# The pitch and the place of the split weight tiles in a two-layer decoder step

## What is computed

```python
def _layer(x, ...):
    x = _layernorm(DN_ALPHA * x + 0.5 * _swiglu(x, ffn1_wg, ffn1_wu, ffn1_wd), ln1_g, ln1_b)
    m, ... = _mixer(x, ...)
    x = _layernorm(DN_ALPHA * x + m, ln2_g, ln2_b)
    x = _layernorm(DN_ALPHA * x + 0.5 * _swiglu(x, ffn2_wg, ffn2_wu, ffn2_wd), ln3_g, ln3_b)

def _swiglu(x, wg, wu, wd):
    return (jax.nn.silu(x @ wg) * (x @ wu)) @ wd

def _mixer(x, ...):
    z = x @ w_in
    cv, cb, cc, lx, lg, q, gl = jnp.split(z, IN_OFFSETS, axis=-1)
    y_conv = (cb * conv3(cc * cv)) @ conv_out
    y_lru = (rg_lru(conv4(lx)) * jax.nn.gelu(lg)) @ lru_out
    y_att = attention(q, k_mem, v_mem) @ att_out
    merged = g[:, :, 0] * y_conv + g[:, :, 1] * y_lru + g[:, :, 2] * y_att
    return merged @ w_o, ...
```

## Time and profile before

| | us |
|---|---|
| median of 3 runs | 1476.64 |
| lowest and highest of them | 1473.49, 1476.66 |
| the profiled execution | 1473.8 |
| its span | 1472.0 |
| PE busy | 1435.8 |
| DVE busy | 880.0 |
| ACT busy | 640.3 |

### The profile page before, as it was taken

One profiled execution on the slowest core, in us unless ns is written; L12 is line 12 of the kernel. 1 busy time (PEld: TensorE's weight loads), 2 busy tenths in 40 slices (PEclk: granted clock), 3 DMA queues, 4 the chain that ended last, 5 costly groups with the idle time before them and its releaser, 6 DMA issues.

```text
span 1472.0 us, 25592 instructions
## 1 busy us (share of the span) xinstructions
PE 1435.8 (98%) x10700; PEld 1420.6 (97%) x10700; DVE 880.0 (60%) x1128; ACT 640.3 (43%) x825; POOL 29.2 (2%) x62
## 2 busy tenths in 40 slices
PE   7999999999999999999999999999999999999996
PEld 7999998999999989999989999999999999999996
DVE  4555557586655775554575555576775557655544
ACT  4444445344334564443464444453623345534433
POOL 1000000000000000000000000000000000000000
PEclk9999999999999999999999999999999999999998
DMA  6444445544535544444444444444454544444451
GB/s 249 169 171 171 158 158 168 193 170 161 211 144 170 196 146 160 156 169 160 171 155 161 169 171 158 158 158 172 147 211 145 188 143 144 172 166 154 168 176 54
DMA packets 39565, 243.60 MB, mean 165 GB/s; under 512 B 4529, under 2 KB 4545, under 8 KB 15809
## 3 DMA queue, kind: packets, MB, share of 16 engines
q1 hardware_dynamic: 32976, 219.30, 42.6%
q0 software_dynamic: 5936, 22.01, 4.2%
q10 hardware_dynamic: 576, 1.18, 0.2%
HBM read 238.97 MB, written 3.50 MB: 165 GB/s over the span
## 4 chain that ended last, share of the span: by engine, by line
PE 91%; DVE 5%; issue 1%; ACT 1%; DMA 1%; DVEq 0%; SPq 0%; ACTq 0%; POOLq 0%
PE ps L370 27%; PE ps L372 27%; PE ps L371 27%; PE ps L542 2%; PE ps L551 2%; PE ps L409 1%; PE ps L414 1%; PE ps L410 1%; DVE wlo L877 1%; DVE y L1026 1%; DVE y L1034 1%; ACT whi L650 1%; DMA raw<-in_ffn_wu 1%; DVE xl L1042 1%; PE ps L557 1%
## 5 line engine op out<-in xcount | busy, mean ns | idle before, releaser
L877 DVE TENSOR_TENSOR wlo<-raw,whi 128x1024 fp32r<-128x1024 f32 x448 | 510.8, 1146 | 372.0 <-ACT whi L650 371.9
L650 ACT CAST whi<-raw 128x1024 fp32r<-128x1024 f32 x448 | 440.1, 985 | 575.6 <-PE ps L372 494.2
L370 PE MATMUL ps<-xh,whi 128*128 128x288 f32 x1984 | 591.3, 298 | 0.2 <-DVE pool L935 0.2
L372 PE MATMUL ps<-xh,wlo 128*128 128x288 f32 x1984 | 586.5, 296 | 0.0
L371 PE MATMUL ps<-xl,whi 128*128 128x288 f32 x1984 | 586.1, 295 | 0.0
L370 PEld LDWEIGHTS ps<-xh,whi 128*128 128x128 f32 x1984 | 373.9, 188 | 1.0 <-issue 0.4
L371 PEld LDWEIGHTS ps<-xl,whi 128*128 128x128 f32 x1984 | 373.9, 188 | 0.6
L372 PEld LDWEIGHTS ps<-xh,wlo 128*128 128x128 f32 x1984 | 373.9, 188 | 0.0
L370 PE MATMUL ps<-hh,whi 128*128 128x288 f32 (+1 forms) x1088 | 323.9, 298 | 0.0
L372 PE MATMUL ps<-hh,wlo 128*128 128x288 f32 (+1 forms) x1088 | 320.0, 294 | 0.0
L371 PE MATMUL ps<-hl,whi 128*128 128x288 f32 (+1 forms) x1088 | 319.8, 294 | 0.0
(11 more groups left out here) (169 smaller groups left out, 881.8 us busy)
## 6 DMA issues: line engine op xcount, KB each, us to landing
raw<-in_w_in SPq DMA_DIRECT2D x48, 1024.0 KB, 4.9
raw<-in_ffn_wu SPq DMA_DIRECT2D x44, 1024.0 KB, 4.8
raw<-in_ffn_wg SPq DMA_DIRECT2D x43, 1024.0 KB, 4.8
raw<-in_ffn_wd SPq DMA_DIRECT2D x32, 1024.0 KB, 4.9
raw<-in_ffn_wd SPq DMA_DIRECT2D x16, 768.0 KB, 4.2
pool<-in_cache_k POOLq DMA_DIRECT2D x16, 512.0 KB, 4.5
pool<-in_cache_v POOLq DMA_DIRECT2D x16, 512.0 KB, 4.8
raw<-in_w_o SPq DMA_DIRECT2D x8, 1024.0 KB, 5.1
```

The costliest lines, as they stand in the source:

```text
L370: mm(out, wh, mh, start=start, stop=False)
L372: return mm(out, wl, mh, start=False, stop=stop)
L650: s_.copy(whi[:, s, k0:k1, :], raw[:, s, k0:k1, :]).then_inc(hi_ready, 1)
L877: return v.tensor_tensor(out, full, high.bitcast(F32), sub)
```

## The change

```diff
@@ -17,6 +17,7 @@
 ATANH_TERMS = 9
 WARM = 20
+SHIFT = 24
@@ -126,8 +127,10 @@
         raw = sb("raw", [P, 2, 8, BC])
-        whi = sb("whi", [P, 2, 8, BC], F32R)
-        wlo = sb("wlo", [P, 2, 8, BC], F32R)
+
+        whi = sb("whi", [P, 2, 8, T], F32R)[:, :, :, 0:BC]
+        wlo = sb("wlo", [P, 2, 8, T], F32R)[:, :, :, 0:BC]
+        sb("shift", [P, SHIFT])
         x = sb("x", [P, KD, T])
```

## The result

| | before | changed |
|---|---|---|
| median, us | 1476.5 (4 runs) | **1463.6** (4 runs, 1461.9 to 1468.2) |
| ratio to before | | **0.9917**, 95% interval 0.9902 to 0.9932 |
| profiled execution, us | 1473.8 | 1468.2 |
| its span, us | 1472.0 | 1466.4 |
| granted clock, share of 2.4 GHz | 0.992 | 0.990 |

The change makes the kernel 0.8% faster, 13 us. My likeliest case, no change at 1476 us, did not come; the time lies in the stated range, and within 1.5 us of what I had given to the rival "the distance counts, and 96 is good".

What follows compares the result with a forecast made beforehand. The matrix engine was taken as the bound, busy 1435.8 of 1472.0 us, so time is matmul count times pace. Splits, loads, pitch and the 96 bytes each counted 0, giving 1476 us, likeliest range 1472 to 1480, overall 1453 to 1489.

Steps and rivals of the forecast that it cites:

- no change at 1476 us: Whole kernel: the layout changes but the matmul pace does not; 1476 us, chance 0.42.
- the distance counts, and 96 is good: 288-column matmuls: all reach the better of two paces, 131.7 ns, giving 1465 us or less; chance 0.36 for better distance.
- 0 for the splits: Weight casts on ScalarE and subtractions on VectorE: unchanged within 2 ns at 1046 and 1223 ns, booked as 0.
- 0 for the loads and the waits: Loads from memory: raw stays, other targets move by 4192 bytes, worth 0; matmul waits of 11.4 us expected unchanged.
- one nanosecond for 0.65%: The 9600 matmuls with 288 columns: one nanosecond on each is 9.6 us, 0.65% of the time.
- the good case: Stream of 48 matmuls: even-odd k step gone, all weight tiles at 0.79 us for six matmuls.
- step 3: Weight pitch: distance becomes the same for all k; worth 0 if only the moving tile's own start counts.
- step 4: The 96 bytes: distance becomes 96 or 224; even and odd k may change roles, mean stays, worth 0.
- reading (a): Even-odd k step of 2.5 ns comes with the distance between moving and weight addresses; bounds 12 us either way.
- reading (b): Even-odd k step of 2.5 ns comes with the moving address alone, whatever the weights do; the change is worth 0.
- rows 6 and 7: Trace paces before the change: 256 columns at 119.3 ns without an even-odd step, 512 columns at 235 ns.
- 2.4 ns lost in each 256 bytes: Moving stream: a loss of about 2.4 ns per 256 bytes read, giving 119, 132.1 or 134.5, and 235 ns.

Runs made afterwards that it cites:

- e6: Changed kernel with 64 bytes between weight and moving tiles in place of 96: 1474.8 us, ratio 0.9982.
- e7: Changed kernel with 128 bytes between weight and moving tiles in place of 96: 1476.1 us, ratio 1.0001.
- e3: Kernel before with 96 bytes added between raw and whi, so weights and moving tiles move together, pitch 1024: 1476.8 us, ratio 1.0004.
- e1: Changed kernel without the 96 bytes, so the weight pitch of 1152 bytes alone: 1469.0 us, ratio 0.9954.
- e4: Kernel before plus 25 blocks of 32 equal, unused matmuls at varied distances, weight widths and column counts; 131.6 to 133.4 ns for 288 columns with 128 weight columns.
- e9: Kernel before plus 52 unused blocks copying its 48-matmul stream at varied distances and weight pitches; moving the weights alone took a block from 6.27 to 6.42 us.

## Why the forecast failed, and where it held

**What held.** That the pace of the matmuls is all that this change can move; 0 for the splits (1048 and 1224 ns after 1046 and 1223); 0 for the loads and the waits; one nanosecond for 0.65% (1.0 ns in the traces makes 9.9 us, 0.67%; the times have 0.8%, with the clock in them); and the rival's price: 1465 us for "all at the better level", 1463.6 measured. By my own criterion of what would show it, the good case came: the step between even and odd k gone. Both are in part luck. At an equal clock the gain is 8 to 10 us and not 12, and the step is gone in e6 and e7 too, at the old pace. That the time lay in the range is owed to the rivals that made it wide, and not to the mechanism that I had forecast from.

**What failed** is the choice in step 3 and with it step 4: between reading (a), the distance, and reading (b), the moving tile's own start, I took (b), "because rows 6 and 7 speak for (b)". Two links were weak.

The first: the earlier trace rows show no step at 256 columns, and I argued that (a) would need one. It needs none of that sign or size: in the table 256 columns are 1.2 ns slower at distance 0, not faster. The effect of a distance depends on how long the stream is beside it, and in the sequence of the kernel it can vanish.

The second: the arithmetic of "2.4 ns lost in each 256 bytes" met 119, 132.1, 134.5 and 235 ns, four numbers with two constants, and I read this as proof. One of the four was not even met: by its starts to 1 ns the 512-column matmul of the earlier trace rows takes 233.1 ns, and it takes 229, 233, 238 and 233 in turn with all operands in place, which no fixed loss per 256 bytes can give. The large part of it is sound in so far as the loss does not go with the width of the weight load (8 weight columns leave it) and does go with the 4-byte elements (bf16 ends it). The step between even and odd k was a separate matter that the same constant happened to fit: e3 keeps the distances and keeps it, e1 keeps the moving starts and all but loses it (0.793 and 0.789 us). e3 would have told the two apart in one run: it moves the tiles' own starts and leaves the distances, and costs nothing.

**Where the rival was right for part of the reasons.** It had two levels and put the new distance at the better one. The levels are no price list per distance: by them e7 would take 1484 us and takes 1476. A layout comes with a few paces of the whole sequence, and 96 bytes at a pitch of 1152 is one whose paces (6.27 to 6.35 us a stream) are all better than 6.37. The gain of both halves (13 and 12 us in the two series) is not clear of the sum of each (7.7, with an interval of 4.4 to 9.2, and 3.4, with 1.6 to 4.4).

**The Trainium skill's rule** that TensorE's two read ports are independent and never wait ("SBUF — State Buffer", section "Who interferes with whom") would have made the change worth 0, as I wrote. The measurement decides: for bf16 no run here contradicts it, at the two distances tried; for float32r the place of the weights alone moves the pace by 1.7 ns in repeated matmuls (e4) and by 3.2 ns in copies of the sequence (130.6 to 133.8 ns in e9).

**What stays open.** By what the matmuls lock, and why in steps of 26.7 ns for 48 of them, no run shows. So the record shows that the operands' places relative to each other set which paces can come, and not how. Nor is it shown what makes a stage take one of several possible paces; that it differs between two executions of one program, and between the two layers in one of them, points to the moment at which the stage begins, but this was not varied. The pause before a stream and the exact order of the three products were left as they are. The paces are known for the profiled executions only, so that the spread of the other runs comes from them is likely, not shown. The 9 ns between float32r and bf16, some nine times the 1.0 ns that the change brought, were not attacked.

## What to carry to other kernels

Where matmuls with 4-byte operands set the time, the pace from start to start is to be read to the nanosecond and by place in the stream: a step that comes back with k is a sign that the operands' places in memory count; an even pace is no sign that they are good (e7). Two layouts that fit one trace equally well are told apart by a kernel that moves both operands together. A search over distances is cheap if it is done with copies of the real sequence, not with one matmul repeated; the winner is then to be timed in the kernel, since one layout can have several paces, and runs are to be compared at the same granted clock when the gain is below 1%.

## What the chip did that I had not expected

- float32r matmuls with 288 moving columns and 128 weight columns took 130.0 to 136.6 ns by the distance between the operands; bf16 took 122.5 to 122.8 at both distances tried.
- The same float32r matmul, repeated with every operand in place, did not take the same time each time: 127, 133, 134, 133 ns in turn at distance 0, and 229, 233, 238, 233 with 512 columns.
- At half clock the same float32r matmul takes its columns alone, 240 ns: the loss exists at 2.4 GHz only.
- Streams of 48 matmuls took 6.267, 6.293, 6.320, 6.347, 6.360 or 6.373 us, and nearly all streams of a stage repeat their value within 1 ns.
- The same program ran the same stage at 6.266 us a stream in one execution and 6.320 in another.
- 512 columns took 227.8 ns at distance 0 and 232.8 at 128; for 256 it was 120.0 and 118.8, the other way round.
